# Fourier products of a token-mixing layer gathered into one block ahead of the rank products, out of the attention tiles

## The reference, cut to what matters

```
def latent_attention(q, k, v, k_ctx, v_ctx, sink):
    ...
    lw = jnp.einsum('bnqhgd,bnkhd->bhgnqk', qb, kw).astype(jnp.float32) * scale
    lw = jnp.where(valid, lw, NEG_INF)
    lc = jnp.einsum('bnqhgd,bchd->bhgnqc', qb, k_ctx).astype(jnp.float32) * scale
    p = softmax_with_sink(jnp.concatenate([lw, lc], axis=-1), sink)
    pw, pc = p[..., :3 * BLOCK], p[..., 3 * BLOCK:]
    out = (jnp.einsum('bhgnqk,bnkhd->bnqhgd', pw.astype(v.dtype), vw)
           + jnp.einsum('bhgnqc,bchd->bnqhgd', pc.astype(v_ctx.dtype), v_ctx))

def fourier_mix(u):
    B, T, _ = u.shape
    ug = u.reshape(B, T, FOURIER_GROUPS, HEAD_DIM).astype(jnp.float32)
    y = jnp.fft.fft2(ug, axes=(1, 3), norm='ortho').real
    return y.astype(u.dtype).reshape(B, T, FOURIER_WIDTH)
```

## Time and profile before

| | |
|---|---|
| median of 2 timed runs | 2245.99 us (2241.59 to 2250.38) |
| the profiled execution: its time, its span | 2258.61 us, 2256.4 us |
| TensorE busy | 2087.6 us, 93% of the span |
| VectorE, ScalarE, GpSimd busy | 1201.6, 694.1, 265.0 us |
| mean granted clock of TensorE | 0.958 |
| the stretch of the change, layer 0 and layer 1 | about 242 to 346 us and 1296 to 1393 us |

### The profile page before, as it was taken

How to read it: one execution, slowest core, us unless ns; L and a number is a source line. 1 busy time by engine, 2 the same in 40 slices (tenths; PEclk the granted TensorE clock), 3 DMA queues, 4 the chain that set the end, 5 groups by cost and what they waited for, 6 DMA issues and landing times.

```text
span 2256.4 us, 48183 instructions
## 1 busy us (share of the span) xinstructions
PE 2087.6 (93%) x20626; PEld 1798.2 (80%) x20626; DVE 1201.6 (53%) x2421; ACT 694.1 (31%) x1194; POOL 265.0 (12%) x377
## 2 busy tenths in 40 slices
PE   6999798889799999999899979888969999999996
PEld 3757577886599999999666767787659999899995
DVE  3458654444466422323456855445166666666664
ACT  3110323331422122121211133342144454444542
POOL 0001224520000000000000204540000110101110
PEclk9999769999899999999999969999989999999998
DMA  8353201001124322220425301000155666656666
GB/s 305 106 203 100 77 3 43 4 5 38 53 97 150 112 75 75 75 66 30 150 98 171 114 33 41 7 4 3 44 197 174 221 211 203 219 204 220 218 195 201
DMA packets 190652, 256.51 MB, mean 114 GB/s; under 512 B 9168, under 2 KB 141728, under 8 KB 190272
## 3 DMA queue, kind: packets, MB, share of 16 engines
q1 hardware_dynamic: 185456, 237.32, 30.5%
q0 software_dynamic: 4992, 16.13, 2.9%
HBM read 239.26 MB, written 16.78 MB: 113 GB/s over the span
## 4 chain that ended last, share of the span: by engine, by line
PE 82%; DVE 7%; issue 3%; ACT 3%; DMA 2%; POOL 1%; SPq 0%; DVEq 0%; ACTq 0%; POOLq 0%
PE bank L972 40%; PE bank L1249 9%; PE bank L963 9%; PE bank L1491 6%; PE bank L946 3%; PE bank L1122 3%; DMA ring<-in_moe_w 2%; PE bank L1219 2%; PE bank L1238 2%; PE bank L933 1%; PE bank L1199 1%; PE bank L896 1%; DVE arena L2401 1%; ACT arena L1668 1%; DVE rms L1951 1%
## 5 line engine op out<-in xcount | busy, mean ns | idle before, releaser
L972 PE MATMUL bank<-g_hi,w_hi 128*128 128x224 f32 (+1 forms) x1376 | 392.8, 285 | 10.1 <-issue 6.3
L972 PE MATMUL bank<-g_hi,w_lo 128*128 128x224 f32 (+1 forms) x1376 | 391.5, 285 | 0.0
L972 PE MATMUL bank<-g_lo,w_hi 128*128 128x224 f32 (+1 forms) x1376 | 391.2, 284 | 0.0
L2139 DVE TENSOR_TENSOR w_lo<-ring,w_hi 128x1024 fp32r<-128x1024 f32 x192 | 232.2, 1223 | 134.2 <-ACT w_hi L1909 134.0
L1249 PE MATMUL bank<-arena 64*64 64x64 f32 (+1 forms) x8640 | 263.3, 227 | 33.1 <-issue 20.3
L1249 PEld LDWEIGHTS bank<-arena 64*64 64x64 f32 x8640 | 247.5, 135 | 47.6 <-issue 26.5
L972 PEld LDWEIGHTS bank<-g_hi,w_hi 128*128 128x128 f32 x1376 | 264.5, 192 | 12.2 <-issue 7.1
L972 PEld LDWEIGHTS bank<-g_lo,w_hi 128*128 128x128 f32 x1376 | 264.5, 192 | 0.2
L972 PEld LDWEIGHTS bank<-g_hi,w_lo 128*128 128x128 f32 x1376 | 264.6, 192 | 0.0
L1909 ACT ACTIVATE w_hi<-ring 128x1024 fp32r<-128x1024 f32 x192 | 202.3, 1060 | 129.5 <-PE bank L972 113.4
L972 PE MATMUL bank<-h_hi,w_hi 128*128 128x320 f32 x704 | 221.2, 314 | 11.5 <-DVE h_lo L2504 11.5
(11 more groups left out here) (296 smaller groups left out, 2920.3 us busy)
## 6 DMA issues: line engine op xcount, KB each, us to landing
ring<-in_moe_w SPq DMA_DIRECT2D x100, 1024.0 KB, 7.0
arena<-in_mod_w SPq DMA_DIRECT2D x40, 1024.0 KB, 5.3
ring<-in_ffn_w SPq DMA_DIRECT2D x30, 1024.0 KB, 7.4
ring<-in_w_in SPq DMA_DIRECT2D x16, 1024.0 KB, 7.5
ring<-in_w_out SPq DMA_DIRECT2D x8, 1024.0 KB, 8.5
ring<-in_mod_w SPq DMA_DIRECT2D x8, 1024.0 KB, 6.1
ring<-in_dft SPq DMA_DIRECT2D x4, 1024.0 KB, 6.8
ring<-in_w_in SPq DMA_DIRECT2D x4, 896.0 KB, 11.0
```

What stands on the lines that cost most here:

```text
L972: ins = mm(out, lhs[x], rhs[y], start=(first and i == 0), stop=(last and i == 2))
L2139: v.tensor_tensor(dst[1], src, f32(dst[0]), ALU.subtract).then_inc(s_lo2, 1)
```

## The change

The Fourier products leave the tiles. All eight groups stand in one block behind `qt` and ahead of the rank products, and all are emptied by ScalarE, ahead of its wait for `s_conv`. Between a tile's scores and its transposes TensorE now has `turn_out` alone. The load of the `dft` table moves in SP's list from behind the loads of the cached keys and values to ahead of them.

```
 def fourier_groups(j):
-    return [[("f1", 0), ("f1", 1)], [("f1", 2), ("f1", 3)], [("f1", 4), ("f2c", 0)], [("f2", 0)], [("f2", 1)]][j]
+    return []
+
+FOURIER_FIRST = [("f1", x) for x in range(NT)] + [("f2c", 0), ("f2", 0), ("f2", 1)]
...
         for j in range(NT):
             order.add(("qt", l, j), "V")
+        for name, x in FOURIER_FIRST:
+            order.add((name, l, x), "A")
...
+                load(("dft", l, 0))
                 order.wait_filled(sp, ("in", l, CF_TILES[-1][0], 1))
                 sp.dma_start(ck_tok, a["cache_k"][0, l].rearrange("t h d -> t (h d)")).then_inc(s_cache, 16)
                 sp.dma_start(cv_tok, a["cache_v"][0, l].rearrange("t h d -> t (h d)")).then_inc(s_cache, 16)
-                load(("dft", l, 0))
...
-                pe.wait_ge(s_rank, 16 * 4 * (l + 1))
-                for h in range(2):
-                    order.wait_emptied(pe, ("in", l, ("wa", 0), h))
...
                 order.wait_emptied(pe, ("ckt", l))
                 for j in range(NT):
                     order.wait_emptied(pe, ("qt", l, j))
...
+                for name, x in FOURIER_FIRST:
+                    fourier(name, x)
+
+                pe.wait_ge(s_rank, 16 * 4 * (l + 1))
...
+                for name, x in FOURIER_FIRST:
+                    take_fourier(name, x)
                 act.wait_ge(s_conv, l + 1)
```

More of the change, by code:

```diff
@@ L1201, in fourier @@
                     end(ins)
+                for name, x in FOURIER_FIRST:
+                    fourier(name, x)
+                pe.wait_ge(s_rank, 16 * 4 * (l + 1))
+                for h in range(2):
+                    order.wait_emptied(pe, ("in", l, ("wa", 0), h))
+                for kind in range(2):
+                    for d in range(2):
+                        for ct in range(2):
+                            for h in range(2):
+                                b = psum[order.open(pe, ("up", l, kind, d, ct, h))]
+                                end(mm(b[:, 0:HALF], rank_up[:, 2 * kind + d, P * ct:P * ct + P],
+                                       waT[:, HALF * h:HALF * (h + 1)], start=True, stop=True))
                 def turn_out(j):
@@ L1734, in _, with take_fourier @@
                         end(ac(tmp[:, ct, HALF * h:HALF * (h + 1)], b[:, 0:HALF], ACT.Sqrt))
+                def take_fourier(name, x):
+                    b = take((name, l, x))
+                    if name == "f1":
+                        end(ac(v1[x].rearrange("p a b -> p (a b)"), b[:, :], ACT.Copy))
+                    elif name == "f2c":
+                        end(ac(mixT[:, 6:8, 0:CTX], b[:, 0:256].rearrange("p (t n) -> p t n", t=2), ACT.Copy))
+                    else:
+                        end(ac(mixT[:, 6 + x, CTX:TOK], b[:, :], ACT.Copy))
+                for name, x in FOURIER_FIRST:
+                    take_fourier(name, x)
                 act.wait_ge(s_conv, l + 1)
@@ L1767, in _ @@
                         decays(j - 1)
[L1768 to L1777, removed]
                     for h in (0, 2):
@@ L2355, in _ @@
                     for name, x in fourier_groups(j):
[L2356 to L2361, removed]
+                        b = take((name, l, x))
+                        end(v.tensor_copy(mixT[:, 6 + x, CTX:TOK], b[:, :]))
                     for h in (1, 3):
```

## The result

| | before | after |
|---|---|---|
| median of the timed runs | 2245.99 us (2 runs) | 2283.39 us (2280.16 to 2286.62, 2 runs) |
| ratio, 95% interval | | 1.0146 [1.0116, 1.0177] |
| profiled execution, span | 2256.4 us | 2278.0 us |
| mean granted clock | 0.958 | 0.959 |

The changed kernel is slower by 1.5%, 37 us. The prediction was 2283 us.

What follows compares the result with a forecast made beforehand. TensorE, 82% of the chain that ended last, was taken as the bound, with its idle times and granted clock. +15.6 us at an unchanged clock plus +21.0 for the clock, on 2246.0, gave about 2283 us, range 2258 to 2301.

Steps and rivals of the forecast that it cites:

- The block in front: From the last `qt` copy to the end of the rank products: 30.6 us against 18.9, +11.7 us a layer, +23.4 in all.
- The five terms: In front, per layer: wait for the `qt` copy 1.6 us, `f1` 5.0, `f2c` 1.0, two `f2` 14.1, rank products 8.9.
- The gaps in the tiles and the clock: Between scores and transposes: shorter gaps in tiles 3 and 4, -5.4 us; the clock falls in each gap where still high.
- the even chance of a rise in the transposes of tiles 2 and 3: Clock rising again at these transposes, one in two each; worth 12.0 us back over both layers.
- -5.4 - 2.4 + 29.0 - 12.0: Tiles, both layers: shorter gaps -5.4 us, copy waits -2.4, clock low throughout +29.0, rises at even chances -12.0.
- The waits of `pv` for copies: In the tiles, `f1` copies no longer delay those `pv` needs: 0.4 us in each of three tiles, -2.4 us in all.
- The recurrent stage, +4 us: After the tiles it begins at the low clock until dense products raise it: 2 us a layer, between 2 and 16.
- The clock never comes back inside the tiles: Rival: clock stays low from tile 0 to the end of the tiles, +48.6 us, 2295 us; chance 0.22.
- The clock does as before: Rival: transposes of tiles 2 and 3 raise the clock in most cases, +15.6 us or some more, 2262 us; chance 0.15.
- Faster than before: Rival: the dense block holds the clock high through all the tiles, -12 us, 2234 us; chance 0.03.
- The recurrent stage stays low: Rival: the first of its five pairs of steps runs at the low clock, 19 us a layer, 2321 us; chance 0.06.
- The sum, +36.6 us: Whole kernel: +15.6 us at an unchanged clock and +21.0 for the clock, set on the median, about 2283 us.

Runs made afterwards that it cites:

- f2_eighth: The changed kernel with one product in place of eight in each `f2`: 2259.21 us, ratio 1.0035 to the kernel before.
- split: Part of the change alone: `f1` and `f2c` in front, the two `f2` left in tiles 3 and 4: 2242.58 us, ratio 0.9986 to the kernel before.
- ranks_first: The changed kernel with the Fourier block behind the rank products in place of ahead of them: 2291.55 us, ratio 1.0194 to the kernel before.
- r_after_2: The changed kernel run again without alteration, its third profile: 2282.68 us, ratio 1.0161 to the kernel before.
- before_fill: The kernel before with 2, 3 and 4 dummy products in the gaps of tiles 0 to 2: 2249.55 us, ratio 0.9994.

## Why the prediction was right, and where it was not

**The block in front, +23.4 us: right, a little short.** Three profiles give +25.5. The five terms were 1.6 (measured 2.0), 5.0 (4.56 or 6.24), 1.0 (1.05), 14.1 (13.97) and 8.9 (8.78). The 2 us that were missing are the dip of the clock behind the wait for the copies, in five of six fronts (1.7 us each, 2.8 over both layers in the mean); the terms differ by less than 0.5 us each otherwise. `f2_eighth` shows that the `f2` cost what they take, `split` that the 6 us of the others cost nothing.

**The gaps in the tiles and the clock.** The falls came as forecast, at each gap that TensorE reached at the high level. The step that was mis-sized is the even chance of a rise in the transposes of tiles 2 and 3: the clock rose behind them in 12 of 12 cases over three profiles, and behind tile 1's twelve transposes in 2 of 6, behind tile 4's twelve in none. For tile 2 of the kernel before the even chance was right: 3 of 6. Why the kernel after differs is open; there the sixteen transposes come behind 6.2 to 6.4 us without work, before behind 3.2 to 4.6. In the forecast the tiles cost +9.2 us over both layers (-5.4 - 2.4 + 29.0 - 12.0); measured were +1.4. Part of that is not the kernel after: the forecast was built on a first profile of before whose layer 0 was 7.6 us slower in the tiles than the five other layers measured. Against that profile alone (163.0 us) the tiles after took 3.6 us less, and the forecast's own terms with all four rises taken as certain give -2.8 (-5.4 - 2.4 + 29.0 - 24.0).

The smaller steps can be read from the profiles, by comparing the time from a tile's scores to its transposes at the same clock level. In tiles 0 to 2 it is the same before and after, as forecast: 4.60 us in tile 0, 10.48 in tile 1 and 13.3 in tile 2 with the scores at the low level. In tile 3 it went from 10.57 to 10.27, in tile 4 from 9.68 to 8.4: 0.3 and 1.3 us in place of 1.6 and 1.1, so -3.2 us over both layers and not -5.4. The 1.6 was read in a tile whose scores, and the start of whose `f2`, ran at the low level. The waits of `pv` for copies, 2.4 us over both layers in the first profile (0.88, 1.16, 0.34), are gone in all three profiles after, as forecast.

**The recurrent stage, +4 us: wrong, nothing.** It took 161.2 us a layer before and 160.5 after, means over three profiles. The clock was low for its first 3 us and then high for most of it. The first 80 records took 3.6 us in place of 2.2, so the low start is there, but the stage as a whole was no longer for it.

**The rivals.** *The clock never comes back inside the tiles* is out, and the rule of the Trainium skill that goes with it ("TensorE: Matmul & The Clock Gate", Part 4: PE-mode transpose), that transposes do not release the clock, does not hold in this kernel: in the kernel after the clock rose behind the sixteen transposes of tiles 2 and 3 in 12 of 12 cases. In the kernel before it was 3 of 6, layer 1 each time; in layer 0 of its three profiles sixteen transposes that ran wholly or mostly at the low level (3.67, 3.09 and 3.08 us) were not followed by a rise. *The clock does as before* came nearest for the tiles. *Faster than before* is out: the dense block did not carry the clock over the 3.9 us gap in any of six layers. *The recurrent stage stays low* is out.

**The sum, +36.6 us: right, in good part by luck.** The timed medians give +37.4, +34.5 and +31.9 us, the three profiles +29.8. The terms measured are 25.5 + 1.4 + 2.9. Against the profiles the forecast had 7.8 us too much in the tiles and 5.4 too much in the recurrent stage (+4, measured -1.4 over both layers), 2.1 too little in front, and nothing for the remaining 4.3, which lie within the scatter of the rest. The mechanism named first carries nearly all of the loss. The errors cancel with one more: the +36.6 were worked out from an execution 12.6 us above the median and then added to the median. Against that execution the mean of the three after is longer by 24.2 us, and 2258.6 + 36.6 would have been 2295. That the medians lie above the profiles' sum by 2 to 8 us I cannot put down to a place, beyond the some 2.5 us that the slow layer 0 of the first profile takes from it: the rest of the same kernel differs by 10 us from one profile to the next.

## What to carry to other kernels

Work that fills a wait is free only up to the length of the wait. Before gathering filler in one place, add it up against the idle time there and against the time it was hiding in: here 20 us went into a wait of 7.6, and came out of gaps where most of it had cost nothing, and where the long `f2` had kept the clock up, worth some 4 us a layer (34.9 us against 30.8 from tile 3's scores on). The same cut that moved only the 6 us that fit was no slower, and with dummy products in the gaps 0.3% faster. Where an engine has two clock levels, a forecast built on one profile should ask how far that execution's clock pattern is typical.

## What the runs showed of the hardware that was not expected

- An idle time of 2.0 us between dense products was followed by a stretch at 0.5 (1.2 GHz) in five of six fronts, at a cost of 1.7 us; two idle times of 1.0 to 1.3 and 1.0 to 1.8 us, with only the transposes between them, were followed by a fall in 5 of 8 cases in the three kernels with dummy products.
- Sixteen float32 transposes of 128 by 128 were followed by a rise from 0.5 to 1.0 in 12 of 12 cases in the kernel after, and in 10 of 10 more in f2_eighth, split and ranks_first; in tile 2 of the kernel before, in 3 of 6. Twelve such transposes, in tiles 1 and 4 of the kernel after, were followed by one in 2 of 12. The scores (64 rows) and the products with the values (64 columns), busy for 11 to 12 us without a break, were not followed by a rise in layer 0 of r_after_2 or in tile 1 of before_fill.
- The recurrent stage's products of 64 by 64 are followed by a rise some 3 us on when they start at the low clock, and the clock then holds for most of 160 us.
